# Prompt attention on one core: the value products moved behind the next scores, the spread of the inverses behind the next head's transposes

## The reference

```python
def forgetting_attn_prompt(q, k, v, logf):
    f_cum = cumsum(logf)                       # per head
    # for each block of 128 queries:
    logits = q @ k.T * HEAD_DIM ** -0.5 + (f_cum[query] - f_cum[key])
    logits = where(query_pos >= key_pos, logits, -inf)
    probs  = softmax(logits)                   # over the keys
    out    = probs @ v
```

## Time and profile before

| | |
|---|---|
| median of 3 runs | 3444.45 us (3444.41 to 3455.21) |
| profiled execution, its own time | 3452.47 us |
| its span | 3450.8 us |
| PE busy | 3194.4 us, 93% of the span |
| DVE busy, ACT busy | 1557.7 us, 823.1 us |
| prompt attention | first scores at 1782.3 us, last spread until 2077.7 us |

### The profile page before, as it was taken

How to read it: one execution, slowest core, us unless ns; L and a number is a source line. 1 busy time by engine, 2 the same in 40 slices (tenths; PEclk the granted TensorE clock), 3 DMA queues, 4 the chain that set the end, 5 groups by cost and what they waited for, 6 DMA issues and landing times.

```text
span 3450.8 us, 52301 instructions
## 1 busy us (share of the span) xinstructions
PE 3194.4 (93%) x20484; PEld 3009.6 (87%) x20484; DVE 1557.7 (45%) x2523; ACT 823.1 (24%) x1417; POOL 258.9 (8%) x363
## 2 busy tenths in 40 slices
PE   7999969999999988899988998879699999999878
PEld 6999959999999978899987774449599999999877
DVE  5434383333443365633334554433734334433662
ACT  3111131111111122312234552222321111111221
POOL 1000000000000000000035432210000000000000
PEclk9999989999999999999999998989899999999989
DMA  2111101111111111013244547861011111111101
GB/s 91 43 49 37 50 19 43 44 49 44 43 44 44 49 56 31 25 43 120 65 124 100 107 83 269 286 236 49 13 49 49 43 43 43 50 43 43 58 28 58
DMA packets 225758, 238.56 MB, mean 69 GB/s; under 512 B 10469, under 2 KB 183525, under 8 KB 225586
## 3 DMA queue, kind: packets, MB, share of 16 engines
q1 hardware_dynamic: 199554, 155.21, 14.8%
q0 software_dynamic: 26032, 80.82, 8.1%
HBM read 201.11 MB, written 18.10 MB: 64 GB/s over the span
## 4 chain that ended last, share of the span: by engine, by line
PE 85%; DVE 6%; DMA 4%; issue 2%; ACT 2%; POOL 1%; POOLq 0%; SPq 0%; DVEq 0%; ACTq 0%
PE psum L1525 19%; PE psum L1523 19%; PE psum L1524 19%; PE psum L1538 5%; PE psum L1544 5%; PE psum L1539 5%; PE psum L1839 2%; DMA kpage<-in_cache_k 2%; PE psum L1823 1%; PE psum L1883 1%; DVE psum L1033 1%; PE psum L1808 1%; DVE y L1039 1%; DVE h L1049 1%; PE psum L1809 1%
## 5 line engine op out<-in xcount | busy, mean ns | idle before, releaser
L1523 PE MATMUL psum<-xs_hi,w_hi 128*128 128x384 f32 (+1 forms) x2736 | 893.0, 326 | 7.3 <-DVE y L1248 4.2
L1525 PE MATMUL psum<-xs_hi,w_lo 128*128 128x384 f32 (+1 forms) x2736 | 892.3, 326 | 0.0
L1524 PE MATMUL psum<-xs_lo,w_hi 128*128 128x384 f32 (+1 forms) x2736 | 891.6, 326 | 0.0
L1523 PEld LDWEIGHTS psum<-xs_hi,w_hi 128*128 128x128 f32 x2736 | 513.6, 188 | 9.3 <-DVE y L1248 5.5
L1524 PEld LDWEIGHTS psum<-xs_lo,w_hi 128*128 128x128 f32 x2736 | 513.6, 188 | 0.0
L1525 PEld LDWEIGHTS psum<-xs_hi,w_lo 128*128 128x128 f32 x2736 | 513.6, 188 | 0.0
L1538 PE MATMUL psum<-xs_hi,w_hi 128*128 128x384 f32 (+1 forms) x1104 | 363.4, 334 | 9.3 <-DVE w_lo L1011 3.7
L1539 PE MATMUL psum<-xs_hi,w_lo 128*128 128x384 f32 (+1 forms) x1104 | 360.8, 331 | 0.0
L1525 PE MATMUL psum<-hid_hi,w_lo 128*128 128x384 f32 (+1 forms) x1056 | 346.0, 328 | 0.0
L1524 PE MATMUL psum<-hid_lo,w_hi 128*128 128x384 f32 (+1 forms) x1056 | 345.1, 327 | 0.0
L1523 PE MATMUL psum<-hid_hi,w_hi 128*128 128x384 f32 (+1 forms) x1056 | 344.7, 326 | 0.0
(11 more groups left out here) (254 smaller groups left out, 3729.0 us busy)
## 6 DMA issues: line engine op xcount, KB each, us to landing
kpage<-in_cache_k SPq DMA_DIRECT2D x64, 512.0 KB, 5.7
v_page<-in_cache_v POOLq DMA_DIRECT2D x64, 512.0 KB, 5.9
raw<-in_w_gate SPq DMA_DIRECT2D x44, 512.0 KB, 3.7
raw<-in_w_up SPq DMA_DIRECT2D x44, 512.0 KB, 3.6
raw<-in_w_down SPq DMA_DIRECT2D x44, 512.0 KB, 3.8
raw<-in_w_in SPq DMA_DIRECT2D x24, 512.0 KB, 3.5
raw<-in_w_ple_gate SPq DMA_DIRECT2D x16, 512.0 KB, 3.5
out<-rows_out POOLq DMA_DIRECT2D x16, 512.0 KB, 2.9
```

The lines of the kernel that those rows point to most:

```text
L1523: M(out, wh, xh, start=first, stop=False)
L1524: M(out, wh, xl, start=False, stop=False)
L1525: return M(out, wl, xh, start=False, stop=last)
```

## The change

On PE the value products of a pair are issued one item later: at odd i, behind the scores of item i+2 and ahead of the transposes of item i, for items i-3 and i-2. Before they were issued at the even item, behind its transposes. The spread of a head's inverses stays at the first item of the next head, but since the last pair's products have moved away, it now follows directly behind that item's transposes; the products of the last pair come behind the scores after it. On DVE `normed` moves from the second to the third item of the next head. ACT, POOL and SP keep their lists.

```diff
@@ -1391,7 +1391,7 @@
             for i in range(NITEMS):
                 if i + 2 < NITEMS:
                     maxes(i + 2)
-                if i % NI == 1 and i > 1:
+                if i % NI == 2 and i > 2:
                     normed(i // NI - 1)
                 take_probT(i)
                 if i % NI == NI - 1:
@@ -1856,13 +1856,13 @@
             for i in range(NITEMS):
                 if i + 2 < NITEMS:
                     scores(i + 2)
+                if i % 2 and i > 1:
+                    outputs((i - 3) // 2)
                 transpose_probs(i)
-                if i % 2 == 0 and i:
-                    outputs(i // 2 - 1)
                 if i % NI == 0 and i:
                     spread(i // NI - 1)
+            spread(H - 1)
             outputs(NPAIRS - 1)
-            spread(H - 1)
```

## The result

The changed kernel took 3456.94 us (median of 15 runs, 3439.31 to 3466.62) against 3445.79 us for the kernel before (15 runs beside it). The ratio is 1.0032, with a 95% interval of 1.0020 to 1.0043. So it is slower in both, by 6 to 11 us. Three executions in a slower state, one each in runs 5 and 8 and one of the kernel before beside them, are left out of the ratios. Whether that lies above the 0.3% line of the forecast, the two measurements leave open. The forecast was 3449.2 us, 4.8 us above the median then known.

A forecast was written before the change was run, and what follows sets the result against it. PE was taken to bound the attention. Per head -1.72 +0.05 +0.30 +1.60 +0.16 = +0.39, over thirteen heads +5.1, less 0.3: +4.8 us on the 3444.45 median, 3449.2 us; 8-in-10 range 3438 to 3461.

The forecast's parts named there:

- What bounds, and where it counts: PE bounds the attention; gains before head 3's first scores are swallowed, except POOL's earlier start, so 13 rounds count.
- the -0.3 of the sum: Before head 3's first scores: POOL's chain starts earlier, between 0 and -0.6 us, -0.3 taken as the middle.
- T0, T1, T4 and O(0,1) for a copy, removed: PE's waits at transposes of items 0, 1, 4 and products of items 0, 1: 1.72 us a head, removed.
- O(0,1) for `o_taken`, added: Products of a head's first pair wait for DVE's `normed`, now behind item 4's maximum: +1.60 us a head.
- X for ACT's copy, added: The spread, behind item 0's transposes, waits until ACT has emptied bank 5 of their first half: +0.30 us a head.
- Openings: Changed starts of product, score and transpose blocks on PE: +0.16 us a head, bounds -0.27 to +0.66; dearer rival, chance 0.08.
- The wait ahead of S1: Item 1's scores might wait for item 7's exponentials: up to 0.2 us a head, 2.6 us, in the range.
- The clock: Rival: clock falls in the new `normed` wait, 6 times some 2.5 us, 15 us more, 3464; chance 0.09.
- The sum: +0.39 us a head, +5.1 over thirteen heads, with -0.3 for head 0: +4.8 us.
- Within 0.3%: The whole kernel's time changes by no more than 0.3%, 10.3 us: chance 0.75.
- The chance of slower, 0.17: Slower by over 0.3%: clock case, half of dearer openings, moves doing nothing, and 0.02 of the forecast.
- The second rival: Rival: `normed` comes in time, so the first pair's products do not wait; 20.8 us goes, 3428; chance 0.06.

The follow-up runs named there:

- runs 5 and 8: 5: second set of runs and second profiled execution of the changed kernel, ratio 1.0018; 8: kernel before with only the spread moved ahead of the last pair's products, 1.0018.
- run 1: Changed kernel with `normed` on DVE put back at the second item, PE's list as changed: 3435.24 us, ratio 0.9954 to the kernel before.
- Run 4: Changed kernel with ACT's copy of the first half of item 0's transposes put ahead of item 1's exponentials: ratio 1.0008 to the kernel before.
- runs 9 and 10: 10: kernel before with only `normed` moved to the third item, 3492.56 us; 9: the same with item 5's scores computed twice more in the wait, 3482.46 us.

## Why the prediction came out as it did

**What bounds, and where it counts: right.** From the first scores of head 0 to the spread after head 3's first scores the stage took 71.4 us before and 71.3 after. So little of the loss arose there, but these two figures flatter the forecast: the spread now has the 1 us of O(6,7) behind it instead of ahead of it. Up to the scores of item 4, which follow both, the stage took 74.1 us before and 74.5 after. POOL did start its chain 1.0 us earlier after the start of the stage (14.6 instead of 15.6 us), more than the 0.6 of the forecast, but head 3's first scores came later, 63.5 us after the start instead of 62.1. With the same order on PE they came at 63.2 us in the second execution and at 62.6 in run 1, so this varies by 0.9 us by itself, and the -0.3 of the sum did not show.

**T0, T1, T4 and O(0,1) for a copy, removed: right.** No such wait is left in the trace after. At 1.72 us a head their size is borne out by run 1, where almost only they are gone: 17.27 less 1.72 is 15.55, and the measured 16.37 exceeds that by the spread's wait of 0.66 and 0.16, the forecast of the openings. One reason was wrong: T4's wait was to go because DVE works off its maximum of item 5 during the new wait for `o_taken`. In run 1 there is no such wait and T4's is gone too; there DVE's maximum of item 5 ends at 1889.18 us, while PE is still in O(0,1), which lasts until T3 at 1890.06. And T1's wait was rather 0.49 than 0.54: behind scores of one block a transpose follows the mask after 0.11 (1895.01 to 1895.12 in the trace before), not 0.06.

**O(0,1) for `o_taken`, added: right in kind and place, 0.15 too large.** S5 starts at 1895.17; with its 0.82 and the opening of 0.09 the product could start at 1896.08 and does at 1897.53: 1.45 us, forecast 1.60. `normed` starts 0.09 before the maximum ends and the product 0.06 after `normed` ends; I had charged nothing for the first and 0.14 for the second. These two are 0.17; the 1.60 of the sum was itself rounded from 3.53 less 1.89, which is 1.64.

**X for ACT's copy, added: the term that was mis-sized.** Forecast 0.30 (and 0.05 for T0's second half), measured 0.66: T0 starts at 1889.22 and takes 1.03 with the opening, so X could start at 1890.25; it starts at 1890.91. The prediction let ACT's copy start when T0's first half ended. But in ACT's list the exponentials of item 1, 1.0 us long, stand ahead of that copy. In the trace after they start only at 1889.18, released by T7 (the bracket there reads PE, L1823), because they write into the one of two `prob` buffers that T7 reads; the copy follows at 1890.18. The row that the prediction used for the copy before the change showed the same: it starts at 1887.50, 1.07 us after T0's first half ended at 1886.43, and what stood ahead of it is this row of the trace before:

```profile
1886.50 1.01 ACT L885 ACTIVATE prob<-psum,nmx 128x896 f32<-128x896 f32 x1 [1.65 <-DVE nmx L1361]
```

There the exponentials waited for DVE's late maximum and O(6,7) covered the delay. The change brought the maximum forward, but O(4,5) stands ahead of T7 as it did before, so the exponentials could start no earlier than T7's end; and it took the cover away from X. Run 4 shows it: with the copy ahead of the exponentials X starts 0.37 us late (1888.55 instead of 1888.18) and 0.29 of the 0.66 is gone. The 0.37 that is left is about the 0.35 of the forecast, which had counted the copy alone.

**Openings: right.** The rest of the round's balance, 17.80 - 17.27 + 1.72 - 1.45 - 0.66, is 0.14, forecast 0.16 (0.09 with 0.49 for T1). The opening of a product behind scores, for which the earlier trace rows had no case, is 0.09: the mask at 1892.21 and the product at 1892.41 in the trace after, 0.20 apart, against the 0.11 from such a mask to a transpose. The Trainium skill ("TensorE: Matmul & The Clock Gate", step-by-step section) has the drain of one matmul overlap the fill of the next; the prediction concluded from it that a change of block might cost nothing, and these rows do not bear that conclusion out. The wait ahead of S1 that the range allowed for did not appear.

**The clock: a rival at 0.09 that came true in part.** It fell in three rounds of the profiled execution and one of the other, not in six, and at 1.65 us a fall, not 2.5. That is 1.6 to 4.9 us of the loss. The prediction had called itself wrong if the granted clock between 1850 and 2080 us was not 1.00, and in this point it was: its sum had nothing for the clock. The rival named the place and the mechanism, and runs 9 and 10 show the mechanism on a wait of 2.1 to 2.2 us; its price was too high. The argument against it, that 1.00 held beside waits of 0.5 and 0.7 us, did not reach to a wait twice as long. The Trainium skill's statement ("TensorE: Matmul & The Clock Gate", PE-mode transpose) that transposes do not count as activity as matmuls do leans the same way as what was seen; no run here changed the transposes, so that part was not tested.

**The sum.** Per round +0.39 was forecast and +0.54 measured. The spread's wait was 0.31 too small and the wait for `o_taken` 0.15 too large, so that the errors partly cancelled; that is luck. The twelve full rounds took 6.5 us more for a forecast of 4.7, the stretches ahead of them and behind them 0.8 for a forecast of 0.1, and the falls 4.9 for nothing: together 12.3 in the stage for a forecast of 4.8, up to rounding. The direction held and the median lies in the range. "Within 0.3%", given three chances in four, is where the second set's 1.0018 lies; the first set's 1.0032 lies just over the line, with an interval on both sides of it. The chance of slower, 0.17, was too low: with a sum of +4.8 and a rival that only adds, the weight should have lain nearer the line.

**What would have made it faster was in the prediction.** The second rival, without the wait for `o_taken`, was priced at 20.8 us below the forecast. Run 1 took that wait away. The changed kernel was 11.2 us above the kernel before beside it (3456.94 - 3445.79), run 1 is 15.0 below (3435.24 - 3450.20): 26.1 in all, of which the falls are 1.6 to 4.9.

## What to carry to other kernels

A moved block covers other waits than before and bares the ones that it covered. For each moved block, list what it no longer covers (here the spread's wait for ACT), read what else stands in the other engine's list ahead of the instruction waited for (here the exponentials of item 1), and which handshakes now have a longer list ahead of them (here `o_taken`, by one maximum). When the other engine's half of the change is one line, measure it by itself: the late multiplication cost 26 us on the new order and 40 on the old, and nothing else in the change depends on it. And a wait that is cheap by its length is not cheap where it lets the clock fall; two waits of 0.7 us did not, one of 1.5 did in one round of six.

## What was not expected of the hardware

The clock fell more often where the one long wait of a round was longer, in a stage that is otherwise full: in none of 84 rounds with waits up to 0.8 us, in 6 of 36 with 1.5 us, in 16 of 24 with 2.2 us. These kernels differ in more than the wait; only runs 9 and 10 differ in nothing but its filling, and whether the length of one wait counts or all the idle time near it, the runs do not separate. The shortest fall lasted 3.4 us and cost 1.65 us. With 1.65 of a 2.1 us wait filled with matmuls whose results are thrown away, the medians of the kernel were 10 us lower, 3482.46 against 3492.56.
